# Values directly behind the scores, gate and output steps at the end of each attention chunk

## What is computed

```python
s = jnp.einsum('brnqkgd,brnjkd->brnkgqj', qs, ks) * SCALE
s = jnp.where(mask[:, None, None], s, -jnp.inf)
lse = jax.nn.logsumexp(s, axis=-1)
p = jnp.exp(s - lse[..., None])
o = jnp.einsum('brnkgqj,brnjkd->brnqkgd', p, vs)
...
alpha = jax.nn.softmax(lses, axis=0)
o = jnp.sum(alpha[..., None] * outs, axis=0)
return (o * jax.nn.silu(z)) @ w_out
```

## Time and profile before

| | us |
|---|---|
| median of 3 runs | 2712.76 (2710.93 to 2716.42) |
| the profiled execution's own time | 2705.96 |
| its span | 2704.2 |
| PE busy | 2581.1 (95% of the span) |
| DVE busy | 1161.4 (43%) |
| ACT busy | 847.3 (31%) |
| POOL busy | 543.4 (20%) |
| mean granted PE clock | 0.978 of full speed |

### The profile page before, as it was taken

One profiled execution on the slowest core, in us unless ns is written; L12 is line 12 of the kernel. 1 busy time (PEld: TensorE's weight loads), 2 busy tenths in 40 slices (PEclk: granted clock), 3 DMA queues, 4 the chain that ended last, 5 costly groups with the idle time before them and its releaser, 6 DMA issues.

```text
span 2704.2 us, 38098 instructions
## 1 busy us (share of the span) xinstructions
PE 2581.1 (95%) x14140; PEld 2365.2 (87%) x14140; DVE 1161.4 (43%) x2469; ACT 847.3 (31%) x2090; POOL 543.4 (20%) x573
## 2 busy tenths in 40 slices
PE   6999999999999979999999999997989999899997
PEld 5999999999988748777999999986878899788885
DVE  7311111111144433211454544342655665677774
ACT  6211111111145532100100000002645566666662
POOL 1010101010002211111222222222222122233332
PEclk9999999999999989999999999997989999999998
DMA  4323232323366544783445464636665655544441
GB/s 157 94 85 94 97 111 83 96 94 112 106 203 186 179 147 148 214 234 114 102 106 130 105 132 103 138 106 187 206 230 188 212 191 184 202 138 153 155 152 65
DMA packets 302675, 387.96 MB, mean 143 GB/s; under 512 B 78253, under 2 KB 227397, under 8 KB 301018
## 3 DMA queue, kind: packets, MB, share of 16 engines
q1 hardware_dynamic: 297402, 342.41, 41.6%
q10 hardware_dynamic: 5152, 44.01, 5.0%
HBM read 266.69 MB, written 163.68 MB: 159 GB/s over the span
## 4 chain that ended last, share of the span: by engine, by line
PE 56%; DMA 2%; DVE 2%; ACT 1%; SPq 1%; issue 1%; POOL 1%; POOLq 0%; ACTq 0%; DVEq 0%
PE p_pair L1148 6%; PE p_pair L1149 6%; PE p_pair L1150 6%; PE p_pair L1112 4%; PE p_pair L1114 3%; PE p_pair L1113 3%; PE p_pair L1848 3%; PE p_tps L1829 2%; PE p_pair L1933 2%; PE p_pair L1934 2%; PE p_pair L1935 2%; PE p_pair L1872 2%; PE p_pair L1874 2%; PE p_pair L1873 2%; DMA g_kv_raw<-scratch_kv_rows 2%; PE g_score L1822 1%
## 5 line engine op out<-in xcount | busy, mean ns | idle before, releaser
L281 PE MATMUL a_pair<-a_ht_hi,a_w_hi 128*128 128x412 f32 (+1 forms) x1280 | 449.0, 351 | 2.0 <-DVE a_ht_lo L450 2.0
L283 PE MATMUL a_pair<-a_ht_hi,a_w_lo 128*128 128x412 f32 (+1 forms) x1280 | 448.1, 350 | 0.0
L282 PE MATMUL a_pair<-a_ht_lo,a_w_hi 128*128 128x412 f32 (+1 forms) x1280 | 448.0, 350 | 0.0
L1148 PE MATMUL p_pair<-p_ht_hi,p_q_hi 128*128 128x416 f32 (+1 forms) x960 | 336.7, 351 | 6.6 <-DVE p_turned L1282 6.6
L1149 PE MATMUL p_pair<-p_ht_lo,p_q_hi 128*128 128x416 f32 (+1 forms) x960 | 336.3, 350 | 0.0
L1150 PE MATMUL p_pair<-p_ht_hi,p_q_lo 128*128 128x416 f32 (+1 forms) x960 | 335.0, 349 | 0.0
L281 PEld LDWEIGHTS a_pair<-a_ht_hi,a_w_hi 128*128 128x128 f32 x1280 | 241.5, 189 | 3.0 <-DVE a_ht_lo L450 2.4
L282 PEld LDWEIGHTS a_pair<-a_ht_lo,a_w_hi 128*128 128x128 f32 x1280 | 241.5, 189 | 1.0
L283 PEld LDWEIGHTS a_pair<-a_ht_hi,a_w_lo 128*128 128x128 f32 x1280 | 241.3, 189 | 0.6
L1341 POOL TENSOR_TENSOR p_q_out<-p_q_out,p_turned 128x416 f32<-128x416 f32 (+1 forms) x120 | 142.2, 1201 | 405.2 <-DVE p_turned L1282 331.6
L1280 DVE TENSOR_TENSOR p_q_out<-p_pair,p_table 128x416 f32<-128x416 f32 (+1 forms) x120 | 93.2, 777 | 275.4 <-PE p_pair L1150 156.2
(11 more groups left out here) (219 smaller groups left out, 5160.8 us busy)
## 6 DMA issues: line engine op xcount, KB each, us to landing
out_cache_kv_g_sample<-cache_kv_g ACTq DMA_DIRECT2D x72, 410.0 KB, 3.6
p_table<-rope_columns SPq DMA_DIRECT2D x60, 416.0 KB, 3.2
scratch_q_tiles<-p_q_out SPq DMA_DIRECT2D x48, 512.0 KB, 5.8
g_q_raw<-scratch_q_tiles SPq DMA_DIRECT2D x48, 512.0 KB, 3.9
scratch_partial<-g_parts SPq DMA_DIRECT2D x32, 520.0 KB, 5.2
g_parts<-scratch_partial SPq DMA_DIRECT2D x32, 520.0 KB, 6.2
a_w_raw<-a_w_in SPq DMA_DIRECT2D x32, 512.0 KB, 5.2
g_rows_hi<-scratch_ht_tiles SPq DMA_DIRECT2D x29, 512.0 KB, 5.2
```

Of the source, the lines that this page charges most:

```text
L281: nc.tensor.matmul(out, hi, ht_hi[:, k, cols], start=(k == 0), stop=False)
L282: nc.tensor.matmul(out, hi, ht_lo[:, k, cols], start=False, stop=False)
L283: last = nc.tensor.matmul(out, lo, ht_hi[:, k, cols], start=False, stop=(k == KT - 1))
L1148: nc.tensor.matmul(out, hi, ht_hi[:, k, cols], start=(k == 0), stop=False)
```

## The change

In the loop over chunks `values(c)` moves from the chunk's end to directly behind `scores(c + 3)` and `turn_keys`. The gate steps, the half output product, the transposes of gated rows in chunk 3 and the sample step now follow it. At `i == 0` the gated transposes still stand ahead of it. Only PE's program changes. No operation and no wait is added or taken away.

```diff
@@ -1968,8 +1968,7 @@
             if i == 0:
                 for half in gated_turns(c):
                     turn_gated(*half)
-                if j is not None:
-                    values(c)
+            values(c)
             for z, k in gate_steps[c]:
                 gate_step(z, k)
             if j is not None:
@@ -1979,8 +1978,6 @@
                     turn_gated(*half)
             if c in sample_in:
                 sample_step(*sample_in[c])
-            if i > 0 or j is None:
-                values(c)
         turn_gated(IN_LOOP, 1)
```

## The result

| | before | with the change |
|---|---|---|
| median of the timed runs | 2713.07 us (2710.93 to 2716.42, 4 runs) | 2743.14 us (2742.01 to 2745.32, 4 runs) |
| ratio | 1 | 1.0111 [1.0093, 1.0128] |
| profiled execution | 2705.96 us | 2744.25 us |
| span, mean granted clock | 2704.2 us, 0.978 | 2742.5 us, 0.974 |

The account below looks back on a forecast made before the run. PE, busy 95% of the span, was taken to bound the kernel. Terms of 11.3 + 0.9 + 10.8 + 5.3 = 28.3 us on the profiled 2705.96 gave 2734.3, and 6.8 us up to the median, 2741 us; range 2720 to 2764.

Parts of the forecast that it names:

- Term 1: Starts of tiles 36 to 47: PE's wait grows 0.94 us each, +11.3 us; drain after the last tile, +0.9 us.
- Waits of 1.7 us ahead of 1848, total 44: Sign of being right: such PE waits ahead of values at starts of tiles 36 to 47, total near 44 us.
- Term 2: Elsewhere, mainly early tiles and tiles 33 to 35: values ask for `add_sums` earlier and wait, +10.8 us net.
- loads hang on values after all: Sign of being wrong: late waits for keys that have grown instead of shrunk; no size given.
- Term 3: Values ahead of fillers in 133 chunks: the second 512-column matmul costs 0.04 us more each, +5.3 us.
- The clock rival: Longer late boundary waits bring PE's clock down, adding 20 to 40 us: 2761 to 2781 us; chance 0.12.
- A clock below 1.00 between 2400 and 2650 us: Sign of being wrong: granted clock lowered in the late tiles, which would point to the clock rival.
- Faster: Sums come free earlier, so PE's 19.2 us of waits not for DMA go: 2694 us; chance 0.05.
- No difference: Every new PE wait is taken up by a later one: about 2714 us; chance 0.06.
- Half the size: ACT's and DVE's rows move forward with PE's, so only the late boundary loss stays: 2725 us; chance 0.17.

Follow-up runs that it names:

- run 5: The change itself, unaltered, timed again on another chip beside the kernel before: 2743.64 us, 1.0135.
- run 1: The changed kernel, but in chunk 3 of tiles 33 to 47 values stay in their old place behind the gated transposes: 2725.83 us, 1.0059 of the kernel before.
- run 3: The changed kernel with DVE's `final` moved behind `add_sums`, into chunk 0 of the next tile: 2726.23 us, 1.0063 of the kernel before.
- run 6: The change in tiles 0 to 31 only, tiles 32 to 47 in the order of the kernel before: 2723.88 us, 1.0066 of that kernel.
- run 2: The change in tiles 32 to 47 only, tiles 0 to 31 as in the kernel before: 2733.02 us, 1.0078 of that kernel.
- Run 7: The changed kernel with ACT's copy of low sums and DVE's `add_sums` moved into the same chunk as the values: 2704.99 us, 0.9999 of the kernel before.
- run 4: The kernel before, values in their old place, with only `final` moved behind `add_sums`: 2698.09 us, 0.9957 of the kernel before.
- run 8: Changed kernel with early sums wherever values are early, old order in chunk 3 of late tiles, `final` behind `add_sums`: 2704.14 us, 0.9981 of the kernel before.

## Why the prediction was right, and where it was off

**Direction and size were right.** 2741 was foretold, 2743.14 measured. By the terms, in the attention of the profiled execution:

| term | foretold (us) | measured (us) |
|---|---|---|
| 1, twelve boundaries | 11.3 | 12 x (0.97 - 0.12) = 10.2 |
| 1, drain | 0.9 | 1.07 - 0.19 = 0.9 |
| 2, the other places | 10.8 | 11.3 |
| 3, the neighbour | 5.3 | 133 x 0.035 = 4.7 |
| low clock behind three boundaries | 0 | 4.7 |
| not assigned | | 0.7 |
| sum | 28.3 | 32.5 |

**That it came within 2 us is in part luck.** The sum left out 4.7 us of low clock. It was added to an execution 6.8 us below its kernel's median, while the change's profiled execution lies 1.1 us above its own. And the medians rose by 30.1 us here but by 36.7 us in run 5. What the runs bear out is a loss of 1.1 to 1.35%, made mostly of these terms.

**Term 1 holds, and its mechanism is shown.** A tile grew by 0.97 us, of which three chunks' neighbour cost is 0.12. The chain measures 3.85 us in both kernels, and PE's own work within it is 0.94 less. Run 1 puts these values back and gets the twelve old waits back, 9.4 us in all as before; run 3 takes one link out and the chain is shorter by 1.20. The drain hangs on the gated transposes too: the wait for the last gated rows is 1.07 us where it was 0.19, and with chunk 3's values kept in place (run 1) it is 0.18. What I had wrong was the look of it. "Waits of 1.7 us ahead of 1848, total 44" came out as 0.35 ahead of the second gated transposes and 1.12 ahead of values, and 33.0 in total. I had overlooked that the second gated transposes wait for the low part of the first half's rows, the link just ahead of `final`. Two pauses also show two pipeline ends as busy time, 3.85 - 1.89 - 1.47 = 0.49 us, against 3.85 - 2.83 - 0.78 = 0.24 before. The price is the same, the label another.

**Term 2 holds in sum, with two entries that I did not foresee.** Tile 17 +1.6 net (foretold 1.8), tile 19 +1.3 (1.6), tile 18 +0.9 (1.1). Tiles 3, 6, 9 and 12 wait 1.26 + 1.66 + 1.09 + 1.21 = 5.2 us (6.0), and the waits for keys behind them, up to tile 16, fell by 3.8, net +1.4 (1.9). The small waits in tiles 21 to 31 are seven of 0.30 us and one of 0.37 instead of nine of 0.4, and with two of 0.4 in tiles 17 and 18 they make 3.3 us (3.6); these are distances between starts, of which the profile shows 0.14 to 0.23 us each as idle time. In tiles 33 to 35 the gated transposes' wait of 3.23 us fell to 1.07, and new ones of 1.26, 0.82 and 0.36 came: +0.3 instead of +0.8.

Tile 17's wait is put down to POOL's part of the values, but the cause is `add_sums` behind DVE's backlog, as foretold: POOL's operation ends at 2116.57 + 0.79 = 2117.36, `add_sums` at 2117.35 + 0.68 = 2118.03, values start at 2118.13. In run 6 the same values start at 2118.02, again 0.10 behind the end of `add_sums`, and POOL's operation only at 2118.11; PE came there later, and its wait is 1.13 us. A releaser's name is a guess where several things are waited for.

The first entry that I missed is the wait for keys in tile 28, 2.80 us where it was 1.38 (+1.4). I had named this as a sign of being wrong: that loads hang on values after all. Here they do not. The load is issued 16.65 us after the start of tile 27 (16.19 before), PE asks for it 20.44 us after that start (19.92 before), so both moved alike. What grew is the time from issue to PE's start, 6.58 us for 5.11. It is 6.00 to 6.58 in runs 1, 5 and 6 as well, but 5.16 in run 3, all with this order in tile 28; why is open. The second is the wait of 1.10 us for `add_sums` ahead of values in tile 47. It is there in every profile with early values and late sums in that chunk (1.10 to 1.12 us in the change and runs 1, 2, 3 and 5) and in none of the others. The measured entries make 1.6 + 1.3 + 0.9 + 1.4 + 3.3 + 0.3 + 1.4 + 1.1 = 11.3.

**Term 3 holds.** From one chunk's scores to the next without a wait it was 3.42 us in chunks with 6 fillers and 4.81 in those with 12; it is 3.46 and 4.84. The second 512-column matmul behind values follows by 2467.21 - 2466.93 = 0.28 us, as in the earlier trace rows. The transposes behind fillers, the pair for which no row stood, give nothing back.

**The clock rival was set apart too sharply from the forecast.** I gave it 0.12 as a case of its own: every boundary loses 1.5 to 3 us, or none does. The runs show both: 3 of 12 boundaries in the first profile, ten of 12 in those of runs 2 and 5. Run 5's 2761.94 us is the rival's lower end of 2761, but 5.2 us of its distance to the first profile lie ahead of the attention. A clock below 1.00 between 2400 and 2650 us was my sign for this rival, and it came. The step that failed is "the granted clock around it is 1.00" taken as a reason to put the price at nothing; it should have been a term of its own, from 0 to 12 x 1.5 = 18 us, with the likely value well inside. The rule that the prediction cites from the Trainium skill (TensorE: Matmul & The Clock Gate, section "A second HAM failure mode: psum-queue depth-cycling") speaks of pauses that come often enough and gives no length. The trace agrees with it for 1.12 + 0.35 us a tile; one pause of 0.78 us in 21.4 us does not bring the clock down.

**The other rivals.** "Faster" fails on the row that I gave against it: `add_sums` follows `final` and not the sums. "No difference" fails since 3.8 us is all that the waits for keys took up. "Half the size" fails on run 6: the early tiles alone cost 0.66%. Run 7 shows what all of these needed: with the sums moved as well, the same change costs nothing.

**What stays open.** What decides how many boundaries have low clock behind them in an execution. Why the load of keys for tile 28 takes longer. 0.7 us of the profile's difference have no row. The clock in the early tiles is no cause that can be seen: it is 0.92 between 1900 and 2100 us where it was 0.95, but it is 0.92 in run 4 too, whose PE program is that of the kernel before, and between 1900 and 2400 us it is 0.95 both before and with the change. Nor is it settled whether run 8 is slower than run 4, and why; its longer waits for keys and term 3 are argued, not shown. One row bears on it: with sums moved in all tiles (runs 7 and 8) the load of keys for tile 28 is issued 17.69 us after the start of tile 27, 1.5 us later than before, so there a load does hang on what was moved.

## What to carry to other kernels

When an operation is moved ahead in one engine's order, move whatever frees its buffer ahead in the other engines' orders too, or the wait just moves with it: alone the move cost 1.1%, with `copy_low` and `add_sums` moved as well 0.0%. Before taking work out of a stretch in which an engine waits, time the chain that sets the stretch's end; work that lies beside such a chain is free where it is and costs its full length elsewhere. Look for what stands in the chain's queues and is wanted by nobody soon: moving the 1.28-us `final` behind `add_sums` gained 0.4%, more than any placing of values did. And where the profile names one releaser of several, look at when each of them ended before you build on the name.

## What the runs showed of the hardware

- The same kernel, with the same boundary waits to the hundredth, had a mean granted clock between 2400 and 2640 us of 0.99 in one execution and 0.94 in another. Its six executions on the chip of run 5 alone took 2732 to 2762 us, with mean clocks of 0.979 to 0.969 over the whole span. PE's busy time in those 240 us was 225.24 and 226.00 us in the two, so the busy time of one profile does not tell which it is.
- A stretch at 1.2 GHz stood behind a boundary with pauses of 0.35 and 1.12 us, 0.63 us of busy transposes between them, at 3 of 12 boundaries in one profile and ten of 12 in two others (runs 2 and 5). It cost 1.55 to 1.60 us each time in the first. Pauses of 0.78 us alone left the clock at 1.00 in all twelve tiles, in every profile that has them (before, runs 1 and 6).
- Low clock shows as busy time, not as waiting: in the same 8 us behind a boundary PE was busy for the whole 8.00 us with 39 matmuls at a clock of 0.83 (run 5) and with 50 at 1.00 (the change's first profile). An account of waits alone misses this.
